# Moving the loads and sums of one gate vector behind the first projection, and PE's modulation pieces behind its units

## The reference

```
mod = silu(c) @ w_ada + b_ada                    # w_ada: 2048 x 12288 (six blocks of 2048)
shift1, scale1, gate1, shift2, scale2, gate2 = split(mod, 6)
h = rms_norm(x) * (1 + scale1) + shift1
p = h @ w_in                                     # 2048 x 4112: Fourier part, q, k, v, output gate, gates
mix = [fourier(p_f), mlstm(q, k, v, gates) * sigmoid(p_o)]
x = x + gate1 * (mix @ w_out)                    # 2048 x 2048
... a gated feed-forward (gate2), then the second layer
```

## Time and profile before

| | us |
|---|---|
| median of three runs | 3567.59 (3566.24 to 3567.82) |
| the profiled execution | 3567.82 |
| its span, first to last instruction | 3566.0 |
| PE busy in the span | 3420.5 (96%) |
| DVE busy | 2015.6 (57%) |
| ACT busy | 1538.5 (43%) |
| POOL busy | 324.9 (9%) |
| weights stage, first unit to last | 48.9 to 287.7 |
| start of out1's first unit | 382.3 |

### The profile page before, as it was taken

The page is one execution under the profiler, slowest core; times in us unless marked ns, Lnnn a source line. Parts: engine busy times, 40 slices in busy tenths (PEclk is TensorE's granted clock), DMA queues, the critical chain, the costliest instruction groups (busy, mean ns, idle before and its releaser), DMA issues.

```text
span 3566.0 us, 45458 instructions
## 1 busy us (share of the span) xinstructions
PE 3420.5 (96%) x18594; PEld 2874.5 (81%) x18594; DVE 2015.6 (57%) x2034; ACT 1538.5 (43%) x1567; POOL 324.9 (9%) x379
## 2 busy tenths in 40 slices
PE   7998889999999999999999899999999999999998
PEld 4774678888888888888888799898888788888886
DVE  2663557775566554444444579895455544444445
ACT  3332346653455443333333455663443443333333
POOL 1000000000000000000000147661000000000000
PEclk9998999999999999999999999999899999999999
DMA  9997667777666666976556656667225555555553
GB/s 355 362 337 289 192 188 226 231 219 225 190 183 191 194 197 177 206 201 198 189 189 189 174 148 159 164 168 248 86 84 200 171 189 190 189 193 189 189 190 140
DMA packets 532585, 713.20 MB, mean 200 GB/s; under 512 B 12872, under 2 KB 349056, under 8 KB 526913
## 3 DMA queue, kind: packets, MB, share of 16 engines
q1 hardware_dynamic: 511616, 643.87, 57.3%
q0 software_dynamic: 16016, 62.66, 6.9%
q10 hardware_dynamic: 4784, 4.27, 0.4%
HBM read 698.94 MB, written 11.80 MB: 199 GB/s over the span
## 4 chain that ended last, share of the span: by engine, by line
PE 80%; DVE 8%; ACT 5%; DMA 4%; issue 3%; POOL 1%; ACTq 0%; SPq 0%; DVEq 0%; POOLq 0%
PE ps L2700 9%; PE ps L2702 9%; PE ps L2701 9%; PE ps L2556 8%; PE ps L2560 8%; PE ps L2557 8%; PE ps L2488 7%; PE ps L2489 3%; DVE w_lo L1448 3%; ACT w_hi L878 3%; DMA stage<-in_w_ada 2%; PE ps L2507 2%; PE ps L2508 2%; PE ps L2509 2%; PE ps L2520 1%
## 5 line engine op out<-in xcount | busy, mean ns | idle before, releaser
L1448 DVE TENSOR_TENSOR w_lo<-stage,w_hi 128x2048 fp32r<-128x2048 f32 x496 | 1144.0, 2307 | 1151.8 <-ACT w_hi L878 1151.2
L878 ACT ACTIVATE w_hi<-stage 128x2048 fp32r<-128x2048 f32 x496 | 949.5, 1914 | 1389.2 <-PE ps L2702 574.3
L2700 PE MATMUL ps<-w_hi,xt 128*128 128x512 f32 x1408 | 552.8, 393 | 3.4 <-DVE xt L1499 1.8
L2702 PE MATMUL ps<-w_hi,xt 128*128 128x512 f32 x1408 | 550.1, 391 | 0.0
L2701 PE MATMUL ps<-w_lo,xt 128*128 128x512 f32 x1408 | 549.8, 390 | 0.0
L2488 PE MATMUL ps<-xt,w_hi 128*128 128x512 f32 x1320 | 471.4, 399 | 6.6 <-DVE w_lo L1448 6.6
L2556 PE MATMUL ps<-w_hi,hid_hi 128*128 128x512 f32 x1152 | 449.6, 390 | 5.8 <-DVE w_lo L1448 5.8
L2557 PE MATMUL ps<-w_lo,hid_hi 128*128 128x512 f32 x1152 | 448.3, 389 | 0.0
L2489 PE MATMUL ps<-xt,w_lo 128*128 128x256 f32 x1320 | 371.0, 281 | 0.0
L2560 PE MATMUL ps<-w_hi,hid_lo 128*128 128x512 f32 x1152 | 354.8, 389 | 0.0
L2700 PEld LDWEIGHTS ps<-w_hi,xt 128*128 128x128 f32 x1408 | 265.7, 189 | 59.1 <-issue 2.3
(11 more groups left out here) (443 smaller groups left out, 4501.4 us busy)
## 6 DMA issues: line engine op xcount, KB each, us to landing
stage<-in_w_in SPq DMA_DIRECT2D x92, 1024.0 KB, 5.8
stage<-in_w_up SPq DMA_DIRECT2D x88, 1024.0 KB, 5.7
stage<-in_ffn_w_gate SPq DMA_DIRECT2D x88, 1024.0 KB, 5.2
stage<-in_ffn_w_up SPq DMA_DIRECT2D x88, 1024.0 KB, 5.1
stage<-in_ffn_w_down SPq DMA_DIRECT2D x88, 1024.0 KB, 5.5
stage<-in_w_ada SPq DMA_DIRECT2D x64, 1024.0 KB, 8.4
stage<-in_w_down SPq DMA_DIRECT2D x44, 1024.0 KB, 5.7
stage<-in_w_out SPq DMA_DIRECT2D x32, 1024.0 KB, 5.5
```

The costliest lines, as they stand in the source:

```text
L878: act.activation(w_hi[:, u % 2 * UNIT:(u % 2 + 1) * UNIT], slot(u % SLOTS), ACT.Copy).then_inc(hi_made, 1)
L1448: dve.tensor_tensor(w_lo[:, part], slot(u % SLOTS), w_hi[:, part].bitcast(F32), ALU.subtract).then_inc(split_made, 1)
L2700: pe.matmul(dst, chunk(xt_hi, k, m), wh, start=k == 0, stop=False)
L2702: last = pe.matmul(dst, chunk(xt_lo, k, m), wh, start=False, stop=k == KC - 1)
```

## The change

Three things are moved; nothing is added or removed.

- POOL issues late pieces 0 and 1 when unit 21 of w_in has been used (`split_used` 24), the rest behind the mask and the row of `mlstm_norm_w`.
- DVE adds late pieces 0 to 7 in the fourth quarter, 8 to 15 in the Fourier part, 16 to 19 in the heads, 20 and 21 before the statistics of h, and 22 to 31 in out1.
- PE's order in the first three quarters becomes SP's order, and in the fourth quarter `ada2(i)` stands behind `in_unit(24 + i)`.

```
 POOL
         pool.wait_ge(S["norm_xhat"], 2)
-        for n in range(20):
-            if n >= 2:
-                pool.wait_ge(S["late_acc"], n - 1)
+        pool.wait_ge(split_used, 24)
+        for n in range(2):
             late_piece(n)
...
-        for n in range(20, 32):
+        for n in range(2, 32):
             pool.wait_ge(S["late_acc"], n - 1)
             late_piece(n)
 DVE
             if i == 0:
                 quarter_lo(q)
-            late(n, 1)
+            if q == 3:
+                late(i, 1)
...
             rest(duo(xt_lo, g), turned_duo(g), duo(xt_hi, g), S["mix_lo"])
+            late(8 + 2 * g, 2)
...
             last.then_inc(S["pt_made"], 1)
+            late(16 + h, 1)
...
         split("out1", 16, 0, 1)
+        late(20, 2)
...
+        late(22, 2)
         for u in range(4, 16):
             split("out1", 16, 0, u)
-            if u == 8:
+            if u < 6:
+                late(16 + 2 * u, 2)
+            elif u == 6:
+                late(28, 4)
+            elif u == 8:
                 copy_sum(7, 0, ADA + 2 * KC + 1)
 PE
         for q in range(3):
-            for i in range(8):
-                for a in ((0,), (1,), (2,), (3, 4), (5, 6), (7,), (), ())[i]:
-                    ada(8 * (q + 1) + a)
-                in_unit(8 * q + i)
-                if i == 2:
-                    norm(0, range(2 * q + 2, 2 * q + 4))
-                elif i == 6:
-                    turn_quarter(q + 1)
-        pe.wait_ge(S["mod_made"], 4)
+            for step in range(16):
+                if step in IN_PLACE:
+                    i = IN_PLACE.index(step)
+                    in_unit(8 * q + i)
+                    if i == 2:
+                        norm(0, range(2 * q + 2, 2 * q + 4))
+                    elif i == 6:
+                        turn_quarter(q + 1)
+                else:
+                    ada(8 * (q + 1) + ADA_PLACE.index(step))
         for i in range(8):
-            ada2(i)
             in_unit(24 + i)
...
+            ada2(i)
```

## The result

| | before | after |
|---|---|---|
| median of four runs, us | 3567.70 (3566.24 to 3568.43) | 3603.57 (3601.20 to 3605.06) |
| ratio | | 1.0100, 95% interval 1.0087 to 1.0114 |
| the profiled execution | 3567.82 | 3599.45 |
| its span | 3566.0 | 3597.7 |

The account below looks back on a forecast made before the run. PE was taken as the bound in the weights stage, DMA just covered. Parts 1 and 2 together +2.4, then +3.3, +0.5, +2.2 and +9.1, sum to +17.5 us on 3567.8: median 3585 us, range 3568 to 3602.

Parts of the forecast that it names:

- Part 1: Weights stage and its start: 24 late pieces leave, sparing bytes, PE's w_ada waits and a half-clock stretch; -9.0 us.
- Rival B: Weights stage limited by transfers after all, so the kernel gets faster, 3555 us; chance 0.07.
- Part 2: Weights stage: PE takes each ada piece one unit later, slots refill later; +11.4 us in three quarters.
- The first loop: Three quarters of the weights stage: unit 4 ready 9.7 us after a2's end, PE there at 7.9; wait 1.8 us.
- Unit 5: Three quarters of the weights stage: its load hangs on a4's slot, ready at 19.2 us, PE there at 17.4; wait 1.8.
- the high bound: Whole kernel: slower landings, a half-clock stretch per quarter, Fourier part, heads and out1 at their high ends; 3603 us.
- rival C: Much slower: each slot wait followed by a stretch at 1.2 GHz, each landing 6.5 us; 3600 us, chance 0.2.
- The fourth quarter: Weights stage, last quarter: about two units between a slot's use and need, so no loss, 1 us at most.
- Part 3: Fourier part: pieces 10 to 13 delay w_ada, +3.3 us; pieces 14 and 15 delay the first scores' sum, +0.5.
- Part 4: Heads: late pieces 18 to 20 load in or just before the w_out stream that limits the chain; +2.2 us.
- Part 5: Out1: ten late pieces through a two-buffer ring delay the fold, with PE idle and a half-clock loss; +9.1 us.
- The rest: Behind out1: nothing changes.

Follow-up runs that it names:

- e2: The kernel after with PE's old order, so only the late pieces moved; ratio to the kernel before 1.0033, span 3580.7 us.
- e3: The kernel after with DVE's sum for PE's first scores ahead of the Fourier part's last two late pieces; ratio to the kernel before 1.0100.
- e7: The kernel after with ada2(i) ahead of in_unit(24 + i) again, in the fourth quarter; ratio to the kernel before 1.0092.
- e12: e2 with late pieces 8 to 19 loading 128 of their 1024 columns, DVE adding as before; ratio to the kernel before 1.0003.
- e9: The kernel after with eight useless matmuls ahead of PE's wait at unit 4 in three quarters; ratio to the kernel before 1.0089.
- e4: The kernel before with POOL's first late pieces held until unit 0 is used and pieces added two units later; ratio to it 0.9987.

## Why the prediction was wrong

The direction was right, and each mechanism that the prediction named was found. Two were not in it: the fourth quarter's wait for g_nat, and the chain of landings in the Fourier part. The time was 18.6 us too low (3585 against 3603.57) and outside the range, by 1.6 us. 14.2 us of this are worked out below; most of the rest is that the profiled execution lies 4.1 us under its median. Step by step:

- **Part 1, the pieces leave the stage: right.** Forecast -6.3 us in the stage and -2.7 at the start; e2 shows -8.2 and -2.5, after -3.5 at the start. The load ahead of unit 0 became 2.6 us shorter (14.45 to 11.83); what the start has beyond it is in the turning of the first sums (3.22 and 1.97 us). The 1.9 us beyond the forecast in the stage are not resolved. Rival B (the stage is limited by the transfers) fell: in e2 PE is busy all the time with the pieces gone, and the stage gains 8.2 us and not 25.
- **Part 2, PE one unit later: the step that failed, by its size.** It had 3.8 us a quarter, "nothing" in the fourth, +11.4 in all with ada 8 and the stage's end. After less e2 has 7.1, 6.6, 6.5 and 3.4 us up to the Fourier start, 23.6. Three terms of the quarter were too small. (1) The first loop: from a2's end to unit 4 it is 10.12 us (68.98 to 79.10), forecast 9.7, and a wait of 2.37, forecast 1.8. (2) Unit 5: its load starts when forecast (7.8 us after a2's end, forecast 7.9), but lands 4.2 us behind the load of a6 where the working had 2.5, the full rate of the earlier trace rows. So unit 5 starts 20.5 us after a2's end (89.50 less 68.98), forecast 19.2. (3) Unit 4 took 7.37 us instead of 5.68, since 3.41 us of it ran at 0.50. That puts a5, on which unit 6 hangs, 1.7 us later. So unit 6 came at 28.5 where the working had 26.1: 2.4 us more, and 3.8 + 2.4 = 6.2 against the 6.5 and 6.6 measured.
- **How much of this is the clock.** Terms 2 and 3 overlap. Without the stretch PE would come to unit 6 at 20.5 + 5.68 + 1.0 = 27.2, an estimate, and the quarter would lose 3.8 + 1.1 = 4.9 us; the one quarter without a stretch (the third of e3) loses 4.6. So about 1 us of the 2.7 missing in a quarter is the loads and 1.5 to 2 the clock. The clock was in the high bound (3 x 1.7) and made up rival C, whose reason against it, "the waits are 1.8 us", did not hold: the longest wait of each of the three quarters was 2.4 to 2.9 us, and each had its stretch at 0.50.
- **The fourth quarter.** Forecast 0 to 1 us; measured 3.4 (after less e2, and after less e7). It was costed with the slots alone. PE's wait there is 2.3 us for g_nat and a stretch at 0.50 follows (264.61). That an ada2 less ahead of a unit uncovers DVE's small operations was not looked at.
- **Part 3, Fourier part: the second miss, 8.9 us for 3.8.** The four pieces were costed by their bytes in SP's stream (4.9 us less the hole), and DVE's additions as hidden in its wait for ecols. But a piece that loads beside SP's stream took 8.2 us in the median there (3.9 to 11.3), one load waits for the adding of the one two before, and the sum for PE stands behind three such turns. The working also had the loads of pieces 10 to 13 alone in this part; 14 and 15 load there too (8.2 and 6.7 us), and DVE was costed with their adding only. The row that said how long a landing can take was on record, a median of 7.1 and a maximum of 11.0; it was used for out1 and not here.
- **Part 4, heads: 0.7 for 2.2.** Right within its range; e3 shows that over half of what the Fourier part is spared (5.9 us) is paid here (3.4).
- **Part 5, out1: right.** 10.7 for 9.1. PE waited 5.3 us ahead of the fold (forecast 4.2). The fold came at 458.0 and not at 442. Of these 16 us the stage has 11.4 and the Fourier part 5.1, the start and the heads take off 0.8 and 1.5, and 2.0 are out1's own (53.1 less 44.8 is 8.3, forecast 6.3). The landings took 3.8 to 6.1 us, 5.0 in the median.
- **The rest.** From the second half of out1 on it is 3127.7 us before and 3126.1 after. Among the fourteen kernels this ranges from 3125.0 to 3130.3 without a step of theirs behind it, so differences of up to 5 us between two spans say nothing by themselves.

Rival C (3600, chance 0.2) came nearest: each quarter had its stretch at 0.50. It took landings of 6.5 us as the rest of the cause; the loads of units 4 and 6, which nothing held up, took 5.4 to 5.8, and what else was lost was lost in unit 5's load, in the fourth quarter and in the Fourier part, which the high bound (3603) had at 0 to 1 us and 0 to 5.

## What to carry to other kernels

An order that consumes a slot later delays the load that reuses the slot, so follow each slot from "used" to "needed" and count what the consumer still has to do in between; if that is less than a landing plus its preparation in a busy stream, the wait is there, and a thinner stream does not pay for it. Cost a load issued beside another queue's stream by its slowest landings in that stretch, not by bytes at full rate, above all where a ring of two buffers chains them. And where the aim is an early start, first hold back only the transfers that compete with it: two here, where the change moved 24.

## What the runs showed of the hardware

- Late pieces (0.5 MB, issued by POOL) landed in 3.8 to 6.1 us in out1 (5.0 in the median), at 240 GB/s in the core's sum, and in 3.9 to 11.3 us (8.2 in the median) when issued from 302 to 347 us, beside SP's stream (369 GB/s). The Trainium skill ("DMA: Bandwidth & Descriptors", Queues, rings and completion order) says that each DMA engine takes turns between the rows of queues that have work. By an estimate from this, with half of the 426 GB/s of the earlier trace rows, a piece would take 1.2 us longer than the shortest one (3.9), about 5.1; the trace's median of 8.2 is 3 us above that, so here the rule alone does not give the time.
- Nor do the bytes: with an eighth of them (64 KB, e12) the pieces issued from 289 to 307 us still took 5.1 to 6.1 us in a stretch at 418 GB/s, and the next two, issued at 315.2 and 316.4, 2.1 us.
- In the weights stage after, each 3.41 us at 0.50 came with one wait of 2.3 to 2.9 us in a PE otherwise busy (80.29 after the wait that ended at 79.10, 264.61 after that at 263.95). The length of the wait alone did not decide it. In e9 a wait of 2.00 us, which ended at 87.88, had a stretch behind it; in the second quarter of after one of 2.01 (unit 4, 141.82) had none, nor had one of 2.09 in e3 (unit 4, 205.37). From 50 to 480 us the mean granted clock was 0.91, against 0.95 before.
- e4 holds a DMA share of 1.00 at 371 GB/s while PE has the clock at 1.00 throughout 49 to 230 us and is busy for 178.4 of the 181 us: here a full queue and a busy PE get on together.
